# Feed forwards of layers 1 to 3 with seven block products, chained in one bank, and the modulation in half units

## The reference, cut to what matters

```
def adaln(cond, w, b):
    m = (jax.nn.silu(cond) @ w + b)[..., None, :]
    return jnp.split(m, 6, axis=-1)
def swiglu(h, wg, wu, wd):
    return (jax.nn.silu(h @ wg) * (h @ wu)) @ wd
...
        fp = swiglu(modulate(yp, mp[3], mp[4]), ffn_wg[layer], ffn_wu[layer], ffn_wd[layer])
        yp = layer_norm(ALPHA * yp + mp[5] * fp, ln_g[layer, 1], ln_b[layer, 1])
```

## Time and profile before

| what | value |
|---|---|
| median of 3 runs | 3642.81 us (3637.96 to 3648.82) |
| the profiled execution | 3643.86 us, its span 3642.1 us |
| TensorE busy | 3347.9 us, 92% |
| VectorE busy | 2463.9 us, 68% |
| GpSimd busy | 1819.6 us, 50% |
| ScalarE busy | 1046.3 us, 29% |
| mean granted clock of TensorE | 0.974 |

### The profile page before, as it was taken

How to read it: one execution, slowest core, us unless ns; L and a number is a source line. 1 busy time by engine, 2 the same in 40 slices (tenths; PEclk the granted TensorE clock), 3 DMA queues, 4 the chain that set the end, 5 groups by cost and what they waited for, 6 DMA issues and landing times.

```text
span 3642.1 us, 72747 instructions
## 1 busy us (share of the span) xinstructions
PE 3347.9 (92%) x30644; PEld 3155.3 (87%) x30644; DVE 2463.9 (68%) x3554; ACT 1046.3 (29%) x2118; POOL 1819.6 (50%) x1441
## 2 busy tenths in 40 slices
PE   7888999999789778889999996999999999999997
PEld 5667899999789678888999995899998777899997
DVE  6666788787872567745875769885667565674556
ACT  4333231011353345542310013310013333252432
POOL 4585456565255655625565552565564222443322
PEclk9999999999899899999999997999999999999998
DMA  7111134443255444332343431344332000222221
GB/s 250 58 53 36 59 128 162 145 141 109 76 178 174 127 99 100 84 100 64 122 156 122 134 110 44 108 153 133 121 119 78 24 18 18 64 71 81 93 67 55
DMA packets 230318, 367.59 MB, mean 101 GB/s; under 512 B 105648, under 2 KB 113008, under 8 KB 229872
## 3 DMA queue, kind: packets, MB, share of 16 engines
q1 hardware_dynamic: 172752, 250.82, 22.9%
...
## 4 chain that ended last, share of the span: by engine, by line
PE 75%; DVE 15%; ACT 3%; issue 3%; DMA 2%; SPq 1%; ACTq 0%; POOL 0%; DVEq 0%; POOLq 0%
PE ps L1184 47%; PE ps L1397 7%; PE ps L1468 4%; PE ps L1606 3%; PE ps L1253 2%; PE ps L1619 2%; PE ps L1637 2%; DVE x L2984 1%; PE ps L1578 1%; DVE m_mx L3292 1%; DVE ps L3537 1%; DVE x L2971 1%; DVE s_T L3536 1%; PE ps L1737 1%; DVE ln_cols L2944 1%
## 5 line engine op out<-in xcount | busy, mean ns | idle before, releaser
L943 POOL TENSOR_SCALAR w_hi<-w_raw 128x1024 fp32r<-128x1024 f32 x292 | 340.6, 1166 | 921.8 <-PE ps L1184 658.1
L2868 DVE SCALAR_TENSOR_TENSOR f_acc<-f_unit,silu_c,f_acc 128x512 f32<-128x512 f32 x532 | 614.4, 1195 | 8.2
L948 POOL TENSOR_TENSOR w_lo<-w_raw,w_hi 128x512 fp32r<-128x512 f32 x292 | 462.5, 1584 | 0.0
L1184 PE MATMUL ps<-f_hhi,w_hi 128*128 128x320 f32 x1968 | 448.5, 309 | 0.0
L1184 PE MATMUL ps<-f_hlo,w_hi 128*128 128x320 f32 x1968 | 448.4, 309 | 0.0
L1184 PE MATMUL ps<-f_hhi,w_lo 128*128 128x320 f32 x1968 | 448.2, 309 | 0.0
L946 POOL TENSOR_TENSOR w_lo<-w_raw,w_hi 128x512 fp32r<-128x512 f32 x292 | 425.3, 1456 | 24.4
L1184 PEld LDWEIGHTS ps<-f_hhi,w_lo 128*128 128x128 f32 x1968 | 329.2, 188 | 0.0
L1184 PEld LDWEIGHTS ps<-f_hhi,w_hi 128*128 128x128 f32 x1968 | 329.1, 188 | 0.0
L1184 PEld LDWEIGHTS ps<-f_hlo,w_hi 128*128 128x128 f32 x1968 | 328.9, 188 | 0.0
L2895 DVE SCALAR_TENSOR_TENSOR x<-ps,mod,x 128x320 f32<-128x320 f32 (+2 forms) x288 | 108.6, 433 | 282.7 <-PE ps L1184 186.4
...
## 6 DMA issues: line engine op xcount, KB each, us to landing
w_raw<-in_w SPq DMA_DIRECT2D x312, 512.0 KB, 3.5
...
```

The source lines that it names most:

```text
L943: nc.gpsimd.tensor_scalar(whi[:, slot, :], raw[:, raw_slot, :], 1.0, 0.0, ALU.mult, ALU.add).then_inc(w_hi_done, 1)
L948: nc.gpsimd.tensor_tensor(wlo[:, slot, half:], raw[:, raw_slot, half:], whi[:, slot, half:].bitcast(F32), ALU.subtract).then_inc(w_split, 1)
L1184: last = mm(ps[:, 2 * b + h, 0:HT], w, r[:, h * HT:(h + 1) * HT], start=kt == 0 and n < 2, stop=kt == KT - 1 and n >= 4)
L2868: last = stt(acc[:, cd, :], unit[:, k, :], by, acc[:, cd, :], ALU.mult, ALU.add)
```

## The change

1. `seven` now runs in layers 1, 2 and 3; `ffn` remains for layer 0. The weights' stream counts anew (`STREAM`), since only 4 chunks of such a layer go through `split`, and semaphores and slots get a base for each layer.
2. In a set, products 0, 2, 4, 5 are added one after another in **one bank** (4 for gate, 7 for up) and 3 and 6 in bank 6, 1 in bank 5. Between two of the chain ScalarE copies the bank's state into a corner (`corner_copied`), and TensorE waits for the copy before it adds the next. VectorE's work on corners falls to three additions. Product 0 of the next set is made ahead of products 5 and 6. The raw quarters are those of products 0, 1 and 5.
3. The modulation is done in 48 **half units** (two k tiles, 4 operations of 128x512, `half_step`) in place of 24 units, one in most sets and 24 + 4 over the down panels; every fourth has the reduction. The loads are issued by ScalarE (`load_half`).
4. The pair's activation is made in four quarter operations, and `g_ahi` of its two tiles is cast in reversed order.

```diff
-LAST_LAYER = DEPTH - 1
-SEVEN_FROM = LAYER_BASE[LAST_LAYER] + C_MIX[MIXER[LAST_LAYER]]
-SEVEN_START = SEVEN_FROM + 4
+SEVEN_LAYERS = (1, 2, 3)
+PLAIN = 4
...
+    order = []
+    for g in range(GROUPS):
+        sets = range(GROUP_SETS[g], GROUP_SETS[g + 1])
+        order.append((sets[0], 0))
+        for s in sets:
+            order += [(s, 1), (s, 2), (s, 3), (s, 4)]
+            if s + 1 in sets:
+                order.append((s + 1, 0))
+            order += [(s, 5), (s, 6)]
+        order += [(("down", g, c), h) for c in range(KD) for h in range(2)]
+    return order
+OPERANDS = operand_order()
...
+HALVES = 48
+SET_HALVES = {_s: 2 if _s == 13 else 1 for _s in range(1, SETS)}
+DOWN_HALVES = {**{(_g, _c): 1 + _c % 2 for _g in range(GROUPS - 1) for _c in range(KD)}, (GROUPS - 1, 0): 2, (GROUPS - 1, 1): 1, (GROUPS - 1, 2): 1}
...
+                    opening, more = s == GROUP_SETS[g], s + 1 < GROUP_SETS[g + 1]
+                    if opening:
+                        if s == 0:
+                            pe.wait_ge(q.sil, q.at.sil + 2)
+                        else:
+                            pe.wait_ge(q.upd, q.at.upd + KD * g - 1)
+                        product(s, 0, corner(s), *plain(0, 0), True)
+                    else:
+                        pe.wait_ge(s7.post, at.post + 3 * s - 2)
...
-                    if s == 0:
-                        pe.wait_ge(s7.tsum, at.tsum + 5)
-                    elif not opening:
-                        pe.wait_ge(s7.post, post - 4)
-                    product(o + 1, 5, *mixed(0), True)
...
+                    product(s, 1, 5, *plain(1, 0), True)
+                    if s == 0:
+                        pe.wait_ge(s7.tsum, at.tsum + 5)
+                    pe.wait_ge(s7.copied, at.copied + 3 * s + 1)
+                    product(s, 2, corner(s), *mixed(0), False)
...
-                    pe.wait_ge(s7.plo, at.plo + pool_lows(o + 4))
-                    pe.wait_ge(s7.first, at.first + s + 1)
-                    product(o + 4, 4, *plain(4, 0), False)
...
+                    if not opening:
+                        pe.wait_ge(s7.post, at.post + 3 * s)
+                    product(s, 3, 6, *mixed(2), True)
+                    pe.wait_ge(s7.copied, at.copied + 3 * s + 2)
+                    product(s, 4, corner(s), *mixed(1), False)
+                    if more:
+                        if not opening and s % 2:
+                            pe.wait_ge(s7.silu, at.silu + 3 * (s // 2) + 1)
+                        elif not opening:
+                            pe.wait_ge(s7.act, at.act + 4 * (s // 2 - 1) + 3)
+                        product(s + 1, 0, corner(s + 1), *plain(0, 0), True)
...
-                    product(o + 5, 6, *mixed(3), False)
...
+                    pe.wait_ge(s7.copied, at.copied + 3 * s + 3)
+                    product(s, 5, corner(s), *mixed(3), False)
+                    pe.wait_ge(s7.post, at.post + 3 * s + 2)
+                    product(s, 6, 6, *plain(1, 1), False)
...
+                def load_half(n):
+                    if n >= HALVES or not ahead:
+                        return
+                    if n >= 2:
+                        act.wait_ge(unit_used, USED_BASE[1] + HALVES * (L - 1) + n - 1)
+                    l, c = unit_source(L, n // 2)
+                    k = 2 * (n % 4)
+                    src = a["ada_w"][l].rearrange("(k p) n -> p k n", p=P)
+                    act.dma_start(m_seven_ada.half[n % 2][:, :, :], src[:, k:k + 2, c * 512:(c + 1) * 512]).then_inc(unit_land[n % 2], 16)
+                def activated(f):
...
+                def pair_activated(p):
+                    act.wait_ge(s7.act, at.act + 4 * p + 3)
+                    activated(2 * p + 3)
+                    act.wait_ge(s7.act, at.act + 4 * p + 4)
+                    activated(2 * p + 2)
...
+                def corner_copied(s, j):
...
+                    act.wait_ge(s7.prod, at.prod + o + 1)
+                    nc.scalar.copy((m.G if gated else m.U)[:, {0: 0, 2: 1, 4: 3}[j], :], ps[:, 4 if gated else 7, 0:HT]).then_inc(s7.copied, 1)
...
-                        high(o + 7)
-                        act.wait_ge(s7.prod, at.prod + o + 1)
-                        nc.scalar.copy(m.p1[:, :], ps[:, 4, 0:HT]).then_inc(s7.first, 1)
+                            act.wait_ge(s7.post, at.post + 3 * s)
+                            af(m.G[:, 0:2, :], m.G[:, 0:2, :], ACT.Silu).then_inc(s7.silu, 1)
+                        after(1)
                         if gated and not opening:
-                            pair_activated(s - 1)
-                        for n in range(8, 12):
-                            high(o + n)
+                            pair_activated(s // 2 - 1)
+                        corner_copied(s, 2)
+                        after(2)
+                        after(3)
+                        corner_copied(s, 4)
+                        after(4)
+                        if more:
+                            corner_copied(s + 1, 0)
+                            after(0, s + 1)
...
+                        after(5)
+                        after(6)
+                        for n in HALVES_OF[s]:
+                            load_half(n + 2)
...
+                def half_step(n):
...
+                    for k in range(2):
+                        for cd in range(2):
+                            by, unit = sc_c[:, 2 * kh + k, cd:cd + 1], m_seven_ada.half[n % 2][:, k, :]
+                            if kh == 0 and k == 0:
+                                last = ts(acc[:, cd, :], unit, by, None, ALU.mult)
+                            else:
+                                last = stt(acc[:, cd, :], unit, by, acc[:, cd, :], ALU.mult, ALU.add)
+                        if k == 0:
+                            ch(last)
+                    last.then_inc(unit_used, 1)
+                    dve.wait_ge(unit_used, used + n + 1)
+                    if kh == 3:
+                        flat = acc.rearrange("p d n -> p (d n)").rearrange("p (b x) -> p b x", x=32)
+                        nc.vector.tensor_reduce(part[:, 32 * (c % 6):32 * (c % 6) + 32], flat, AX.X, ALU.add, apply_transpose=True).then_inc(unit_red, 1)
+                        dve.wait_ge(unit_red, RED_BASE[L] + c + 1)
...
                         if more:
                             weight_sums(s + 1)
                         if gated_set and not opening:
-                            act_low(2 + s - 2)
...
+                            pair_low(s // 2 - 1)
+                        dve.wait_ge(s7.copied, at.copied + 3 * s + 1)
+                        done(1)
+                        tt(D[:, 0, :], D[:, 0, :], ps[:, 5, 0:HT], ALU.add).then_inc(s7.post, 1)
+                        if not gated_set:
+                            dve.wait_ge(s7.post, post + 1)
+                            dve.wait_ge(s7.silu, silus + 3)
+                            tt(U[:, 0, :], U[:, 0, :], G[:, 0, :], ALU.mult).then_inc(s7.act, 1)
...
+                            sum_low(s + 1, 3)
+                        for n in HALVES_OF[s]:
+                            half_step(n)
+                        dve.wait_ge(s7.copied, at.copied + 3 * s + 3)
+                        tt(D[:, 3, :], D[:, 3, :], ps[:, 6, 0:HT], ALU.add).then_inc(s7.post, 1)
+                        if not gated_set:
+                            dve.wait_ge(s7.post, post + 2)
+                            stt(U[:, 3, :], U[:, 3, :], -1.0, G[:, 3, :], ALU.mult, ALU.mult).then_inc(s7.act, 1)
...
+                            done(5)
+                            stt(U[:, 2, :], ps[:, 7, 0:HT], -1.0, G[:, 2, :], ALU.mult, ALU.mult).then_inc(s7.act, 1)
...
+                        done(6)
+                        tt(D[:, 1, :], D[:, 1, :], ps[:, 6, 0:HT], ALU.add).then_inc(s7.post, 1)
+                        if not gated_set:
+                            dve.wait_ge(s7.post, post + 3)
+                            tt(U[:, 1, :], U[:, 1, :], G[:, 1, :], ALU.mult).then_inc(s7.act, 1)
+                    pair_low(s // 2)
```

563 lines of the change are left out of this document (297 added, 266 removed).

## The result

The changed kernel takes **3750.46 us** (median of 4 runs, 3746.58 to 3755.61), the kernel before 3645.82 us in the same comparison: a ratio of **1.0288, 95% interval 1.0268 to 1.0309**, or about 105 us more. I had forecast 3690, in a range to 3735: the direction was right, the size less than half of what came. The profiled execution has a span of 3748.9 us and a mean granted clock of 0.961, where before showed 0.974.

What follows compares the result with a forecast made beforehand. TensorE's matmul count was taken to set the time of the three long feed forwards. Terms of -50, +16 and +81 gave +47 us on 3643.9, or 3690 us after 1.1 us for the median; range 3618 to 3735 us.

Steps and rivals of the forecast that it cites:

- Term 1: Layers 1 and 2: 240 fewer TensorE matmuls each, less layer 3's 3.4 us end, 2 x -25.0 = -50 us.
- Term 2: Layer 3's chain: TensorE waits for ScalarE's copy, 2.2 us in 7 gate sets; 16 us with up sets and group openings.
- Term 3: Layers 1 and 2: copy waits plus VectorE's half units delaying corners, reductions, panels and the end, 2 x 40.5 = +81 us.
- rival 3: Slow matmuls behind 21 stands on the copy, 1.5 us each, 3721 us; chance 0.19 together with the bad bounds.
- Rival 1: Half units hide, as GpSimd's operations and VectorE's SBUF work miss each other: 3628 us; chance 0.20 with milder losses around it.
- rival 2: Only the matmul count speaks, as ScalarE reaches the copy in time: -50 us, 3593 us; chance 0.09.
- the two waits: TensorE waits on ScalarE's copies, near 2 us per gate set, all three layers; then on VectorE's corner, layers 1 and 2 alone.

Runs made afterwards that it cites:

- e11: Changed kernel with ScalarE's chained copy before its cast and no half units, so the modulation of layers 2 and 3 is missing: 3610.55 us, 0.9906 of the kernel before.
- e1: Changed kernel with ScalarE copying the chained bank before the cast that waits for the weight sums: 3717.58 us, 1.0201 of the kernel before.
- e12: Changed kernel with ScalarE's chained copy before its cast and the chained form in layer 3 alone: 3649.35 us, 1.0014 of the kernel before.
- e2: Changed kernel without half units, their loads and sums, so the modulation of layers 2 and 3 is missing: 3670.77 us, 1.0069 of the kernel before.

## Why the prediction was right and wrong

- **Term 1, −50 us.** Without half units and copy waits layers 1 and 2 are 449.0 and 448.8 us (e11), against 469.7 and 469.6 plain: −20.7 and −20.8, **−41.5 together**. The count of matmuls was right. I took the end from layer 3, 3.4 us, and in layers 1 and 2 it is 6.83 us even without half units; that is 6.9 of the 8.5 us missing.
- **Term 2, +16 us.** Layer 3 lost **22.5**: 15.9 us of idle time and 6.6 us of slow time. ScalarE's order was the cause (e1 takes 20.4 of it away; 2 to 3 us the chained form costs anyway, e1 and e12). The waits came as I had worked them out, with GpSimd's operation on the first weight sum (the row below; the next sums take 0.68 to 0.70 us). That their sum is so near to 16 is in part luck: the seven waits were 1.72 us and not 2.2, and one of 2.67 us, for a copy in the layer's first set, was in none of my steps. The slow time I had at nothing.

```profile
3353.36 1.80 DVE L3234 TENSOR_TENSOR ps<-g_raw 128x512 f32<-128x512 f32 x1
```

- **Term 3, +81 us.** Measured **+124.2**: 20.3 and 20.4 us for the chain (e2 less e11; I had 17.4), and 45.8 and 37.7 us for the half units (after less e2; I had 23.1 a layer). Of the half units' part in layer 1, idle time ahead of the last panels is 47.4 less 22.5 of e2, 24.9 us; slow time 23.7 less 8.9, 14.8 us; the end 4.0 us; the last panels, with 16 matmuls more, 2.1 us. The waits behind half units were near my figure: 11.5 and 5.3 us on the gate sets' corner where I had 9.1 and 4 for the reductions. Set 13 with its two half units, 3.9 us, was in none of my steps, and the group openings took 7.3 and 6.1 us where I had 4 a layer. The end of 10.85 us is near the 9.4 that terms 1 and 3 gave it.
- **The step that failed** is that the sum held only waits. Over the three whole stretches TensorE's idle time grew by 125.4 us, its slow time by 50.8, and its matmuls fell by 71.0 (2 x 242 at 0.1468 us): 105.2 in sum. The forecast missed by 104.6 − 47 = 58 us. So 51 of the 58 are slow time, which the terms had at nothing: 29 at the lower clock and 22 at the edges of the stands. Some 7 are waits that came longer than priced. I had slow matmuls only as rival 3, 3721 us: 21 stands on the copy at 1.5 us each. The 1.5 us was my estimate from the opening of layer 3, where behind a stand of 4.64 us the twelve matmuls of a product began over 3.10 us for 11 x 0.1468 = 1.61, at a granted clock of 0.52 (3208.80 to 3212.20 of that trace); no row and no run shows it as the price of a stand on a copy. Most of those on the copy did not: behind six of the eight in layer 1 (1.72 us four times, 1.94 and 1.95) the slow time up to the next stand is 0.3 us each. In the same layer three stands on the gate sets' corner (1.92, 2.18, 3.26 us), the one in set 13 (3.94) and those at the two group openings (4.34, 2.91) brought 1.8 to 2.4 us each. Since these were my own later waits, rival 3 was no alternative to the forecast but a part of it. That its 31 us is near the 29 at the lower clock is luck, since most of them come from other stands.
- **Rival 1** (half units hide) and **rival 2** (only the count) fell: a mean of 965 ns for the half unit's operation, and 24 copy waits. Of the signs that I had named for being right, the two waits came where I had put them; the lengths did not come: layers 1 and 2, put near 480 us, read 504.2 and 496.1 up to their ends, and layer 3, put at 456, read 462.4. The waits told the mechanism; only the lengths told that the sum lacked a term.
- **Costed at nothing and right:** the opening (5.1 for 5.5 us), the half units' loads (VectorE waited 1.8 us for them in all), the weights' stream and ScalarE's extra casts (no wait of TensorE in the feed forwards on a load or on a cast of weights stands among the longer ones).
